# Cutting the first loads into parts, splitting weights two units ahead, widening one-column sums: a float32 network of two stacks on one Trainium2 core

## The reference

```python
qkv = jax.nn.silu(_dwconv(concatenate([q, k, v], -1), conv_w))   # five taps, centred
q = _l2norm(to_heads(q)) * (DN_DK ** -0.5)     # t * rsqrt(sum(t * t) + 1e-6)
k = _l2norm(to_heads(k))
```

## Time and profile before

| | us |
|---|---|
| median of 3 runs | 3929.32 |
| lowest, highest | 3927.19, 3929.78 |
| the profiled execution, its own time | 3931.74 |
| its span in the profile | 3929.9 |
| TensorE busy in the span | 3796.0 |

### The profile page before, as it was taken

One profiled execution on the slowest core, in us unless ns is written; L12 is line 12 of the kernel. 1 busy time (PEld: TensorE's weight loads), 2 busy tenths in 40 slices (PEclk: granted clock), 3 DMA queues, 4 the chain that ended last, 5 costly groups with the idle time before them and its releaser, 6 DMA issues.

```text
span 3929.9 us, 43107 instructions
## 1 busy us (share of the span) xinstructions
PE 3796.0 (97%) x17694; PEld 3086.3 (79%) x17694; DVE 2039.7 (52%) x2512; ACT 1093.2 (28%) x1193; POOL 69.1 (2%) x81
## 2 busy tenths in 40 slices
PE   9999999989999999999999999999999999999997
PEld 8878888756788878888777678888888776878886
DVE  5564434553654435434664764434443756575442
ACT  3242222342422222222333222222222242322221
POOL 0000000000000000000010000000000102000000
PEclk9999999998999999999999999999999999999998
DMA  3212222100222222223302222222222313112221
GB/s 135 102 70 96 96 94 100 59 32 36 82 95 98 97 81 95 97 91 123 106 27 81 86 75 96 96 100 94 96 94 99 129 53 97 65 65 96 96 91 70
DMA packets 66788, 343.01 MB, mean 87 GB/s; under 512 B 23524, under 2 KB 23524, under 8 KB 30816
## 3 DMA queue, kind: packets, MB, share of 16 engines
q1 hardware_dynamic: 60864, 303.19, 21.8%
q0 software_dynamic: 5792, 37.92, 2.6%
HBM read 324.31 MB, written 16.78 MB: 87 GB/s over the span
## 4 chain that ended last, share of the span: by engine, by line
PE 86%; DVE 9%; ACT 2%; issue 1%; DMA 1%; SPq 0%; DVEq 0%; ACTq 0%
PE ACC L986 25%; PE ACC L988 25%; PE ACC L987 25%; PE ACC L1617 1%; PE ACC L1351 1%; DVE BX L2867 1%; DVE BT L2865 1%; PE ACC L1331 1%; PE MIX L1263 1%; DVE WL L2274 0%; DVE PT L3054 0%; DVE PT L3056 0%; DMA RAW<-wall 0%; PE MIX L1160 0%; PE ACC L1649 0%
## 5 line engine op out<-in xcount | busy, mean ns | idle before, releaser
L986 PE MATMUL ACC<-HH,WH 128*128 128x512 f32 (+1 forms) x3322 | 1308.2, 394 | 28.6 <-issue 15.3
L988 PE MATMUL ACC<-HH,WL 128*128 128x512 f32 (+1 forms) x3322 | 1291.0, 389 | 0.0
L987 PE MATMUL ACC<-HL,WH 128*128 128x512 f32 (+1 forms) x3322 | 1290.9, 389 | 0.0
L2274 DVE TENSOR_TENSOR WL<-RAW,WH 128x2048 fp32r<-128x2048 f32 x292 | 668.3, 2289 | 481.2 <-ACT WH L1785 480.7
L986 PEld LDWEIGHTS ACC<-HH,WH 128*128 128x128 f32 x3322 | 627.2, 189 | 179.0 <-issue 35.9
L987 PEld LDWEIGHTS ACC<-HL,WH 128*128 128x128 f32 x3322 | 627.2, 189 | 131.3 <-issue 5.3
L988 PEld LDWEIGHTS ACC<-HH,WL 128*128 128x128 f32 x3322 | 626.7, 189 | 129.6
L1785 ACT ACTIVATE WH<-RAW 128x2048 fp32r<-128x2048 f32 x292 | 556.6, 1907 | 559.7 <-PE ACC L988 554.6
L2369 DVE TENSOR_TENSOR SG<-ACC,RS 128x512 f32<-128x512 f32 x132 | 91.3, 692 | 628.6 <-PE ACC L988 628.4
L986 PE MATMUL ACC<-HIDH,WH 128*128 128x512 f32 x1056 | 410.8, 389 | 0.0
L987 PE MATMUL ACC<-HIDL,WH 128*128 128x512 f32 x1056 | 410.8, 389 | 0.0
(11 more groups left out here) (503 smaller groups left out, 3033.4 us busy)
## 6 DMA issues: line engine op xcount, KB each, us to landing
RAW<-wall SPq DMA_DIRECT2D x261, 1024.0 KB, 4.7
RAW<-wall SPq DMA_DIRECT2D x24, 768.0 KB, 4.1
KR<-spectra POOLq DMA_DIRECT2D x4, 2048.0 KB, 9.0
x_kept<-X POOLq DMA_DIRECT2D x2, 2048.0 KB, 7.1
FWK<-mats POOLq DMA_DIRECT2D x4, 1024.0 KB, 5.4
spectra<-SQ POOLq DMA_DIRECT2D x8, 512.0 KB, 3.0
spectra<-T POOLq DMA_DIRECT2D x8, 512.0 KB, 3.8
X<-x_kept POOLq DMA_DIRECT2D x2, 2048.0 KB, 14.1
```

Source lines behind the costliest of these rows:

```text
L986: pe.matmul(out_ap, wh, hh, start=first, stop=False)
L987: pe.matmul(out_ap, wh, hl, start=False, stop=False)
L988: return pe.matmul(out_ap, wl, hh, start=False, stop=last)
L2274: v.tensor_tensor(WL[n % 2][:], RAW[n % 2][:], WH[n % 2][:], ALU.subtract).then_inc(w_lo, 1)
```

## The change

What it does, by part:

1. **Opening.** SP issues, in this order: `PAR`; the first half of unit 0 (its tiles for chunks 0 to 3); X chunks 0 and 1; the second half of unit 0; X chunks 2 and 3; X chunks 4 to 7; then unit 1 as before. POOL waits for X chunks 2 and 3 before it loads `CON`, and for unit 1 before it loads `MEM` and the pool weights. ScalarE and VectorE split the two halves of unit 0 one by one, the second between chunks 1 and 2 of their `HH` and `HL` work. ScalarE first does a one-column copy that needs no data. TensorE does 26 fillers instead of 62, waits for the first half at block 0, for the second at chunk 4, and for `CON` at block 1.
2. **Five-tap stage.** ScalarE's and VectorE's split in block j (0 to 4) is of unit n + 2 instead of n + 1. VectorE's stands behind the copy to `CVT` instead of ahead of it, in blocks 1 to 4 (block 0 keeps its place).
3. **Query and key sums.** Each of the 32 products moves 128 columns of ones and writes 128 columns, of which the next product overwrites all but the first.
4. **End.** 15 fillers ahead of the last sums and 12 behind them, ahead of the spreading product; VectorE waits after every second scaling operation only; X leaves in four stores of two chunks, each issued when its chunks are scaled.
5. **Semaphores.** Seven of the memory norm become three, eight of the mLSTM gates become two; order and waits are the same.

The diff, cut to its core:

```diff
@@ block.sync
-            sp.dma_start(X[:], xT).then_inc(x_landed, 16)
+            sp.dma_start(PAR[:], params).then_inc(par_landed, 16)
+            sp.dma_start(RAW[0][:, 0:8 * P], wall[0:1, :, 0:8 * P]).then_inc(half_landed, 16)
+            sp.dma_start(X[:, 0:2, :], xT[:, 0:2, :]).then_inc(x_landed[0], 16)
+            sp.dma_start(RAW[0][:, 8 * P:], wall[0:1, :, 8 * P:]).then_inc(w_landed[0], 16)
+            sp.dma_start(X[:, 2:4, :], xT[:, 2:4, :]).then_inc(x_landed[1], 16)
+            sp.dma_start(X[:, 4:8, :], xT[:, 4:8, :]).then_inc(x_landed[2], 16)
...
-            sp.wait_ge(block_done, n_blocks)
-            sp.wait_ge(norm_done, stages[-1].plain + (stages[-1].kind == "rms"))
-            sp.dma_start(out, X[:]).then_inc(out_done, 16)
-            sp.wait_ge(out_done, 16)
+            for k in range(KD // 2):
+                sp.wait_ge(out_ready, k + 1)
+                sp.dma_start(out[:, 2 * k:2 * k + 2, :], X[:, 2 * k:2 * k + 2, :]).then_inc(out_done, 16)
+            sp.wait_ge(out_done, 16 * KD // 2)
@@ block.gpsimd
-            pool.dma_start(PAR[:], params).then_inc(par_landed, 16)
-            pool.dma_start(CON[:], consts).then_inc(par_landed, 16)
+            pool.wait_ge(x_landed[1], 16)
+            pool.dma_start(CON[:], consts).then_inc(con_landed, 16)
+            pool.wait_ge(w_landed[1], 16)
@@ pe_linear
-                            pe.wait_ge(w_lo, n + add + 1)
+                            first_unit = isinstance(i, int) and n + add == 0
+                            if first_unit:
+                                pe.wait_ge(half_lo, 1)
+                            else:
+                                pe.wait_ge(w_lo, n + add + 1)
+                            if first_unit is False and isinstance(i, int) and n + add == 1:
+                                pe.wait_ge(con_landed, 16)
...
                                     pe.wait_ge(h_ready, st.hin + k + 1)
+                                    if first_unit and k == 4:
+                                        pe.wait_ge(w_lo, 1)
@@ pe_norm
                 if st.paired and not st.late:
+                    if st.gain == "final2":
+                        keep_clock(MIX[:, 2, :], 15)
                     sum_paired(st)
...
                 if not st.late:
+                    if st.gain == "final2":
+                        keep_clock(MIX[:, 2, :], 12)
                     late_scale(st)
@@ pe_prep
-                            mm = pe.matmul(MIX[:, 2, 4 * m + tc:4 * m + tc + 1], src[:, tc * P:tc * P + P], ONES[:, 0:1],
+                            mm = pe.matmul(MIX[:, 2, 4 * m + tc:4 * m + tc + P], src[:, tc * P:tc * P + P], ONES[:],
@@ block.tensor, opening
-            keep_clock(ACC[:, 0, :], 62)
-            pe.wait_ge(par_landed, 32)
+            keep_clock(ACC[:, 0, :], 26)
@@ act_linear
+                                if st.out == "conv5":
+                                    if i * 2 + j < st.nb - 1:
+                                        split_hi(n + 2, add, i)
+                                    continue
@@ late_hi
                 for c in range(first, end):
...
+                    if st.b0 == 0 and c in (0, 2, 4):
+                        act.wait_ge(x_landed[c // 2], 16)
+                    if st.b0 == 0 and c == 2:
+                        act.wait_ge(w_landed[0], 16)
+                        act.activation(WH[0][:, 8 * P:], RAW[0][:, 8 * P:], ACT.Copy).then_inc(w_hi, 1)
@@ block.scalar, opening
-            split_hi(0, 0, 0)
+            act.activation(PRE[:], ONES[:, 0:1], ACT.Copy)
+            act.wait_ge(half_landed, 16)
+            act.activation(WH[0][:, 0:8 * P], RAW[0][:, 0:8 * P], ACT.Copy).then_inc(half_hi, 1)
@@ dve_linear
-                                if st.opens and isinstance(i, int) and i == 0:
+                                if st.out == "conv5" or st.opens and isinstance(i, int) and i == 0:
                                     continue
...
                             v.tensor_tensor(CVT[:, j], two, scale2, ALU.mult).then_inc(block_done, 1)
+                            if st.out == "conv5" and 0 < i * 2 + j < st.nb - 1:
+                                n, add = unit_of(st, i, j)
+                                split_lo(n + 2, add, i)
                             v.wait_ge(cv_center, cv)
@@ late_chunks
                 for c in range(first, end):
+                    if st.b0 == 0 and c == 2:
+                        v.wait_ge(w_hi, 1)
+                        v.tensor_tensor(WL[0][:, 8 * P:], RAW[0][:, 8 * P:], WH[0][:, 8 * P:], ALU.subtract).then_inc(w_lo, 1)
+                    if st.b0 == 0 and c in (2, 4):
+                        v.wait_ge(x_landed[c // 2], 16)
@@ dve_rms
-                    step(v.scalar_tensor_tensor(X[:, c, :], X[:, c, :], par(st.gain, c), MIX[:, 1, :], ALU.mult, ALU.mult))
-                v.tensor_copy(RN[:, 5, 0:1], EPSC[:]).then_inc(norm_done, 1)
+                    scaled = v.scalar_tensor_tensor(X[:, c, :], X[:, c, :], par(st.gain, c), MIX[:, 1, :], ALU.mult, ALU.mult)
+                    if st.gain == "final2" and c % 2:
+                        scaled.then_inc(out_ready, 1)
+                    else:
+                        step(scaled)
@@ block.vector, opening
-            v.wait_ge(par_landed, 32)
-            split_lo(0, 0, 0)
+            v.wait_ge(par_landed, 16)
+            v.wait_ge(half_hi, 1)
+            v.tensor_tensor(WL[0][:, 0:8 * P], RAW[0][:, 0:8 * P], WH[0][:, 0:8 * P], ALU.subtract).then_inc(half_lo, 1)
```

More of the change, by code:

```diff
@@ L497, in build @@
         rs_at = (nc.sbuf_usable_end - 4 * S) // 32 * 32 - 4 * S
-        assert low + 4 * 2 * KF * S <= rs_at
+        PRE = place("PRE", [P, 1], at=low + 4 * 2 * KF * S)
+        assert low + 4 * 2 * KF * S + 32 <= rs_at
         EV_YA = put("EV_YA", [P, 4, S])
@@ L561, in build @@
         par_landed = sem("par_landed")
-        x_landed = sem("x_landed")
+        con_landed = sem("con_landed")
+        half_landed = sem("half_landed")
+        half_hi = sem("half_hi")
+        half_lo = sem("half_lo")
+        x_landed = [sem(f"x_landed{i}") for i in range(3)]
         mem_landed = sem("mem_landed")
@@ L863, in _ @@
         def _(sp):
-            sp.dma_start(X[:], xT).then_inc(x_landed, 16)
+            sp.dma_start(PAR[:], params).then_inc(par_landed, 16)
[4 more added lines that the diff above has]
+            sp.dma_start(X[:, 4:8, :], xT[:, 4:8, :]).then_inc(x_landed[2], 16)
             def load(st, i, j):
                 n, add = unit_of(st, i, j)
+                if isinstance(i, int) and n + add == 0:
+                    return
                 if not (isinstance(i, int) and n + add < 2):
@@ L1193, in memory_sums @@
                                        start=(c == 0 and mc == 0), stop=(c == KD // 2 - 1), skip_group_check=True)
-                mm.then_inc(mem_summed, 1)
+                mm.then_inc(mem_pe, 1)
             def memory_scale():
-                pe.wait_ge(mem_diag, 1)
-                pe.matmul(MIX[:, 1, 0:M_MEM], ONES[:], DIAG[:, 0:M_MEM], start=True, stop=True).then_inc(mem_scale, 1)
+                pe.wait_ge(mem_dve, 2)
+                pe.matmul(MIX[:, 1, 0:M_MEM], ONES[:], DIAG[:, 0:M_MEM], start=True, stop=True).then_inc(mem_pe, 1)
             def pe_even(st):
                 pe.wait_ge(mem_landed, 32)
-                pe.wait_ge(mem_scaled, 1)
+                pe.wait_ge(mem_dve, 3)
                 for at, g in enumerate(EVEN_ORDER):
@@ L2403, in period @@
                             if i == 1:
[L2404 to L2405 removed]
+                                v.wait_ge(mem_act, 1)
+                                v.tensor_tensor(MSQ[:, 0:4, :], MSQ[:, 0:4, :], MSQ[:, 4:8, :], ALU.add).then_inc(mem_dve, 1)
                             if i == 2:
```

86 lines of the change are left out of this document (39 added, 47 removed).

## The result

The changed kernel is faster. Its four runs have a median of 3897.73 us (3891.97 to 3898.90), against 3929.55 us for four runs of the kernel before: ratio 0.9916, with an interval of 0.9899 to 0.9933. That is 31.8 us gained. The time is 13.7 us above the forecast of 3884, and lies above the range (3878 to 3894). The profiled execution is the fastest of the four, with 3891.97 us and a span of 3890.2, where before the profiled one had 3931.74 and 3929.9. So the two profiles lie 39.8 us apart. The mean granted clock rose from 0.980 to 0.987.

A forecast was written before the change was run, and what follows sets the result against it. TensorE, busy 97% of the span, was taken as the bound. Gains of 11.9 + 15.4 + 12.8 + 5.1 = 45.2 us gave a profiled time of 3886.5, carried to a median of 3884 us; range 3878 to 3894.

The forecast's parts named there:

- The step from the profiled execution to the median: Whole kernel: profiled execution taken as 2.4 us above the median shown, so 3886.5 carried to 3884 us.
- Five-tap stage, forecast 15.4: Both layers: splits two units ahead remove TensorE's standstills and the slow products behind; 15.4 us gained, bounds 11 and 17.
- Behind block 5 the old order remains, with its small wait.: End of the five-tap stage: split order unchanged there, only a small wait expected; no separate size given.
- Opening, forecast 11.9: Start to sums of squares: 36 fewer fillers and loads in parts start them at 26.3; 11.9 us gained, bounds 8.5 and 13.
- Nothing is late, by 1 us at chunk 2: Opening: operands for every chunk are ready before TensorE wants them, with 1 us to spare at chunk 2.
- Query and key sums, forecast 12.8: Both layers: 128 columns cost no more and keep the higher clock; 6.4 us each, 12.8 gained, bounds 6 and 13.5.
- End, forecast 5.1: Last part: split stores 3.0, fewer waits and the copy 0.5, fillers 1.6; 5.1 us gained, bounds -3 and 6.
- They should hold the higher level: End: fillers keep TensorE's higher clock, so four sums take 0.94 instead of 1.87 and L1160 1.04 instead of 2.08 us.
- Each part of a transfer pays alone: Opening: transfers in a row at lone prices put unit 1 at 25 instead of 14.4; about 3893, chance 0.05.
- The lower clock comes anyway: Sums and end: lower clock despite the change, 12.8 lost and 1.6 becomes a small loss; about 3899, chance 0.04.
- The opening is late by a few us: Opening: X parts move at the pace of POOL's small transfers, or granted clock comes later; about 3889, chance 0.10.
- It does not do what it says: TensorE is held elsewhere, so the 4.64 us standstill only moves, and the rest likewise; 3929, chance 0.02.

The follow-up runs named there:

- e6: Changed kernel with GpSimd's two operations on the filter weights made to wait until the five-tap stage is over; median 3892.50 us, ratio 0.9901.
- e3: Kernel before the change with the five-tap splits alone; median 3916.47 us, ratio 0.9970.
- e5: Changed kernel with the two-ahead split carried through block 5, so the next stage's first block splits none; median 3885.19 us, ratio 0.9892.
- e4: Kernel before the change with 128 columns in the query and key sums alone; median 3916.42 us, ratio 0.9976.
- e11: Kernel of e10 with ScalarE's split of unit 0's second half put ahead of the wait for X chunks 2 and 3; median 3880.72 us, ratio 0.9880.
- e8: Kernel of e5 with the parameters' transfer issued on GpSimd's queue instead of SyncE's; median 3884.74 us, ratio 0.9889.
- e1: Changed kernel run again with no edit; median 3891.75 us, ratio 0.9909.
- e9: Changed kernel run a third time with no edit; median 3895.99 us, ratio 0.9921.
- e7: Changed kernel without the 15 and 12 filler products of the end; median 3897.21 us, ratio 0.9920.
- e10: Changed kernel with the edits of e5 and e6 together; median 3882.91 us, ratio 0.9887.

## Why the prediction was right and wrong

The direction was right, and so was what each part does in its own place; the time was 13.7 us short, and outside of the range. Three terms make that up. Against the sum of 45.2 the two profiles show 39.7: 5.5 us. The step from the profiled execution to the median was to give 2.4 us more and gave nothing. And the runs that weren't profiled were slower than the profiled one: 3897.73 - 3891.97 = 5.8 us.

**Five-tap stage, forecast 15.4, measured 8.9.** The step that failed is "Behind block 5 the old order remains, with its small wait." The part on the six blocks was right: no idle time in them. But the reckoning took VectorE's taps at the one price of 6.26, where block 2 had 6.88 before already. It counted 1.1 us to spare in each block, and not that VectorE enters the stage behind TensorE, so that this room was needed to catch up (e6: 0.48 us left at the last copy). And it looked at the margin within the six blocks only. I had not asked what runs on GpSimd when the taps start earlier: its product on the filter weights, which waits for a load, now falls beside taps. Before it fell beside a split, a copy and a wait (1872.18 to 1875.34 us, taps from 1875.63). That costs VectorE 2.82 us in block 2. VectorE regains about 1.25 us in each block that follows (copies 9.63 apart instead of 10.88), then waits 1.40 at the last one, and its split lands 2.4 us too late, at a place where it has no margin. The idle time and the products at 0.50 behind it are the missing 3.3 us per layer; of these, 1.7 us in layer 1 come and go with the execution. e3 shows that this part does it alone, e6 that GpSimd's work is the cause of the long taps, e5 that with the split ahead of the taps the same delay costs nothing. Against the changed kernel e5 regains 8.65 us, more than the 6.5 that were missing, in part because the forecast had kept the small wait there (0.54 us in e6).

**Opening, forecast 11.9, measured 10.5**, and against the opening of e3 and e4 8.8: the forecast's 1.7 us for the stretch at 0.50 hangs on the one execution that it was read from, and that these came in was luck. Mis-sized: the landings. "Nothing is late, by 1 us at chunk 2" rested on parts landing 1.25 us apart from 4.9 us on. They landed 1.2 to 2.3 us later, which used up that 1 us and more; the first product was 0.3 us late, the gap at chunk 2 took about 0.9. The forecast had let ScalarE's half split start at 8.7, with X chunks 2 and 3, although it put the second half at 7.4: in the code the split stands behind the wait for X, which ended last, and I had taken this order over without pricing it. e11 shows the cost by taking it away: the sums then start at 26.69, 0.4 us from the forecast 26.3. That PAR ahead of the first half costs anything (e8) isn't shown. Why the first parts are slow stays open; other sizes, and other queues for the large parts, were not tried. In the traces X in one piece moves in packets of 16 KB and the parts in packets of 4 KB, but the later 388 GB/s were reached with packets of 4 KB too.

**Query and key sums, forecast 12.8, measured 12.5**, and 12.5 alone (e4): right, by its own steps. 128 columns cost no more than one, at 0.228 us for a sum, and the 0.50 behind the sums is gone. The growth with the columns that the Trainium skill lets a matmul have (TensorE: Matmul & The Clock Gate, Back-to-back issue gap) doesn't appear in these records.

**End, forecast 5.1, measured 5.7** in the first profile, and 4.1 in e1 and e9: right within its bounds, in part by luck. L1172, formerly L1160, takes 1.02 us (1.04 forecast), and the stores 2.6 us each (3.0). Without the fillers the end gains 4.2 (e7; 3.5 forecast). The fillers bring 1.5 (1.6 forecast) in three of eight executions and cost 0.1 in five. "They should hold the higher level" is the step that doesn't hold.

**The rivals.** Of *Each part of a transfer pays alone* little came: unit 1 was there at 16.2, not 25. *The lower clock comes anyway* fell for the sums by the windows, and came true for the end in five of eight executions. *The opening is late by a few us* had the right mechanism and about a third of its size (1.4 of 5 us). *It does not do what it says* came true in a small part: the idle time moves on to the next stage, at half its length. No rival had priced that.

**The step from profile to median and the range.** The prediction took an execution noise of 2 us. The kernel before ranges from 3922.57 to 3939.86 in the runs of these groups, and e10 from 3875.65 to 3892.98. The time goes with the granted clock: the kernel before has 3923.23 us at 0.982 and 3937.32 at 0.978 on one chip, e10 3875.65 at 0.989 and 3892.98 at 0.986. At 0.987 about 2 x 0.013 x 3890 = 101 us of the span run at 0.50 (107 by the list of stretches), before 2 x 0.020 x 3930 = 157 (160). Which short stretches these are differs from one execution to the next. Therefore one profile doesn't give the median to better than some 6 us, and the range ought to have been that much wider. The range was also narrower than its own terms: their lower bounds add up to 8.5 + 11 + 6 - 3 = 22.5 us gained, which is 3907, and the text stopped at 3894.

## What to carry to other kernels

When an operation is moved earlier on VectorE, lay GpSimd's instructions over its new place: the same taps cost 6.25 or 9.07 us by what runs beside them. Ask too whether an engine enters the stage on time, before its spare time in each block is counted as a margin. Follow a removed standstill past the end of its stage, to the first operand that is still prepared in the old order; here that one move (e5) brought as much as the stage's whole first gain. And in an order written by hand, put a wait directly ahead of the instruction that needs it: a split that stood behind a wait for other data cost up to 1.2 us.

## What the runs showed of the hardware

VectorE and GpSimd hold each other up, at times for most of an instruction. The first two of block 2's eight taps in the changed kernel, in the timeline:

```profile
1864.08 4.35 DVE L2353 SCALAR_TENSOR_TENSOR DQ<-CVT,PAR,DQ 128x510 f32<-128x510 f32 x2
```

They take 2.91 and 1.41 us, where one takes 0.75 and the next six do. The first starts 0.22 us after GpSimd's product, and ends 0.55 us after it: it waited through nearly all of it. The Trainium skill, page SBUF — State Buffer, section Who interferes with whom, has this rule: a VectorE instruction with two inputs in SBUF contends with a GpSimd instruction that reads SBUF, the port pair that they share is an exclusive lock, and issue order decides who blocks. By that rule the first tap had to wait, and the trace agrees. But the second tap, beside GpSimd's scaling of 3.09 us, lost only 0.66 us, not 3, and the six behind it nothing, although the scaling still ran beside the first of them: there the trace doesn't agree with a block for the whole instruction.

GpSimd pays as well. Alone its two operations take 2.40 and 2.82 us (e6), beside the taps 2.58 and 3.09. Beside a low split, which takes 2.28 us alone, whoever starts second pays for nearly all of what is left of the first. In layer 1 of the changed kernel GpSimd's product starts 0.4 us behind a split and takes 4.15 us. In e9 it starts 0.27 us ahead of one, and there the split takes 4.28 us; the scaling, which starts while that split runs, takes 4.70.

The first loads in parts move slowly: between 3.5 and 6.5 us seven transfers in a row on one queue moved 209 GB/s, in the next 3 us 388. With X in one piece, the same stretch before moved 424 GB/s, and only 0.5 to 3.5 us was slow (120).

Busy work of TensorE doesn't always hold the granted clock. In five of eight executions it fell to 0.50 among 12 fillers that followed 15 others and four sums, with 1.04 us of idle time ahead of the sums; in the other three, where it held, the engine had done the same.
